# Attention with panel filler: one stretch of filler behind turn, outputs, scores and the second turned group

## The reference

```python
z = jnp.einsum('bhqd,bhkd->bhqk', q_blk, kh).astype(jnp.float32) * inv_sqrt
mask = key_pos[None, :] < q_pos[:, None]
log_1m_beta = jnp.where(mask, jax.nn.log_sigmoid(-z), 0.0)
suffix = lax.cumsum(log_1m_beta, axis=3, reverse=True) - log_1m_beta
a = jnp.where(mask, jnp.exp(jax.nn.log_sigmoid(z) + suffix), 0.0)
return jnp.einsum('bhqk,bhkd->bhqd', a, vh.astype(jnp.float32)).astype(q.dtype)
```

## Time and profile before

| | |
|---|---|
| Median of three runs | 2811.23 us |
| The profiled execution, its own time | 2811.8 us |
| Its span | 2810.0 us |
| PE busy | 2688.0 us, 96% of the span |
| PEld, DVE, ACT, POOL busy | 77%, 62%, 41%, 19% |
| The stage, 1481 to 1888 us: PE busy | 405.31 of 407 us |
| The stage: DVE, ACT busy | 202.35, 145.56 us |

### The profile page before, as it was taken

One profiled execution on the slowest core, in us unless ns is written; L12 is line 12 of the kernel. 1 busy time (PEld: TensorE's weight loads), 2 busy tenths in 40 slices (PEclk: granted clock), 3 DMA queues, 4 the chain that ended last, 5 costly groups with the idle time before them and its releaser, 6 DMA issues.

```text
span 2810.0 us, 39071 instructions
## 1 busy us (share of the span) xinstructions
PE 2688.0 (96%) x15746; PEld 2169.7 (77%) x15746; DVE 1731.8 (62%) x1998; ACT 1139.4 (41%) x2138; POOL 541.7 (19%) x434
## 2 busy tenths in 40 slices
PE   7999998999799999999799999999998999999997
PEld 6887566877788887888677777778877788888886
DVE  3467544563787778888815554531245765578889
ACT  3323564333777763333423333331016433333332
POOL 4322001348200000000432222213366000000002
PEclk9999999999999999999899999999999999999999
DMA  3210000004265655322411111221252323343323
GB/s 134 59 31 18 7 4 24 3 25 178 93 202 188 210 170 193 111 87 99 148 55 46 38 46 31 66 80 51 75 198 102 111 100 120 120 150 120 120 105 120
DMA packets 222604, 269.50 MB, mean 96 GB/s; under 512 B 16455, under 2 KB 158046, under 8 KB 222430
## 3 DMA queue, kind: packets, MB, share of 16 engines
q1 hardware_dynamic: 208174, 217.26, 23.9%
q10 hardware_dynamic: 14256, 49.81, 4.5%
HBM read 210.42 MB, written 56.62 MB: 95 GB/s over the span
## 4 chain that ended last, share of the span: by engine, by line
PE 80%; DVE 10%; POOL 3%; ACT 2%; issue 2%; DMA 2%; SPq 0%; ACTq 0%; DVEq 0%; POOLq 0%
PE ps L1647 7%; PE ps L1648 7%; PE ps L1649 7%; PE ps L1702 5%; PE ps L1704 5%; PE ps L1703 5%; PE ps L1761 4%; PE ps L1217 3%; PE ps L1219 3%; PE ps L1218 3%; PE ps L1763 3%; PE ps L1762 3%; PE ps L1438 3%; PE ps L1344 2%; PE ps L1236 1%
## 5 line engine op out<-in xcount | busy, mean ns | idle before, releaser
L1702 PE MATMUL ps<-down_t_hi,down_s_hi 128*128 128x512 f32 x896 | 349.5, 390 | 4.4 <-DVE acc L3205 2.2
L1704 PE MATMUL ps<-down_t_hi,down_s_lo 128*128 128x512 f32 x896 | 348.7, 389 | 0.0
L1703 PE MATMUL ps<-down_t_lo,down_s_hi 128*128 128x512 f32 x896 | 348.6, 389 | 0.0
L1043 POOL TENSOR_SCALAR mean_sq<-ssq 128x1 f32<-128x1 f32 x64 | 37.1, 580 | 1294.7 <-ACT squares_junk_ffn L1921 1242.2
L428 POOL TENSOR_TENSOR slab_lo<-raw,slab_hi 128x1024 fp32r<-128x1024 f32 (+2 forms) x108 | 256.1, 2371 | 9.0
L2385 ACT CAST down_s_hi<-down_a 128x2048 fp32r<-128x2048 f32 x56 | 107.2, 1915 | 370.4 <-PE ps L1704 328.1
L425 POOL TENSOR_SCALAR slab_hi<-raw 128x1024 fp32r<-128x1024 f32 (+2 forms) x108 | 114.6, 1061 | 624.0 <-issue 479.6
L1647 PE MATMUL ps<-act_hi,up_hi 128*128 128x512 f32 (+1 forms) x544 | 205.7, 378 | 6.1 <-issue 2.8
L1648 PE MATMUL ps<-act_lo,up_hi 128*128 128x512 f32 (+1 forms) x544 | 204.9, 377 | 0.0
L1649 PE MATMUL ps<-act_hi,up_lo 128*128 128x512 f32 (+1 forms) x544 | 204.8, 376 | 0.0
L1702 PEld LDWEIGHTS ps<-down_t_hi,down_s_hi 128*128 128x128 f32 x896 | 168.2, 188 | 42.6 <-issue 8.0
(11 more groups left out here) (365 smaller groups left out, 6173.0 us busy)
## 6 DMA issues: line engine op xcount, KB each, us to landing
down_a<-hid_spill SPq DMA_DIRECT2D x32, 1024.0 KB, 7.3
hid_spill<-up_hid ACTq DMA_DIRECT2D x30, 1024.0 KB, 6.4
raw<-in_w_in SPq DMA_DIRECT2D x56, 512.0 KB, 3.8
w_ada<-in_w_ada SPq DMA_DIRECT2D x48, 512.0 KB, 3.9
raw<-in_w_out SPq DMA_DIRECT2D x32, 512.0 KB, 3.8
up_raw<-in_w_up SPq DMA_DIRECT2D x16, 1024.0 KB, 5.4
down_b<-in_w_down SPq DMA_DIRECT2D x16, 1024.0 KB, 6.9
up_raw<-in_w_mlp_in SPq DMA_DIRECT2D x16, 1024.0 KB, 5.4
```

What stands on the lines that cost most here:

```text
L1702: pe.matmul(out, ops["s_hi"][:, k, cols], ops["t_hi"][:, k, :], start=first, stop=False, skip_group_check=True)
L1703: pe.matmul(out, ops["s_hi"][:, k, cols], ops["t_lo"][:, k, :], start=False, stop=False, skip_group_check=True)
L1704: mm = pe.matmul(out, ops["s_lo"][:, k, cols], ops["t_hi"][:, k, :], start=False, stop=last, skip_group_check=True)
```

## The change

In PE's `sb_step` the filler no longer stands in three pieces. Before: first turned group, three units, second turned group, two units, outputs, scores, the rest of the units. Now: first turned group, outputs, scores, second turned group, all six or seven units. No instruction is added or removed, no wait is changed, and the code of the other engines is the same.

```diff
                 if step >= SB_LAG_TURN:
                     pair, item = divmod(step - SB_LAG_TURN, SB_ITEMS)
                     sb_turn(pair, item, 0)
-                    mid_units(unit, unit + 3)
-                    if sb_pieces(item) == 2:
-                        sb_turn(pair, item, 1)
-                    mid_units(unit + 3, unit + 5)
-                    unit += 5
                 if step >= SB_LAG_PV and s % 2 == 0:
                     pair, item = divmod(step - SB_LAG_PV, SB_ITEMS)
                     sb_outputs(pair, item // 2)
...
                     elif s % SB_ROUND == 3 and i + 1 < SB_PAIRS:
                         sb_scores(i + 1, 0, 0)
+                if step >= SB_LAG_TURN and sb_pieces(item := (step - SB_LAG_TURN) % SB_ITEMS) == 2:
+                    sb_turn((step - SB_LAG_TURN) // SB_ITEMS, item, 1)
                 mid_units(unit, end)
```

## The result

| | before | after |
|---|---|---|
| Median (8 runs each) | 2810.77 us | 2818.35 us |
| Ratio, with its 95% interval | | 1.0026 (1.0016 to 1.0036) |
| The profiled execution's span | 2810.0 us | 2816.9 us |
| Step 2 to step 65, first transpose to first transpose | 392.30 us | 398.68 us |
| First transpose of step 2 to the first matmul of the next stage | 397.78 us | 405.03 us |

The changed kernel is slower by 7.6 us, 0.26%. The stage alone grew by 7.25 us in the profiled executions. What lies ahead of it took 0.7 us more and what lies behind it 1.0 us less, both without a change in the code. Steps that an edit does not touch repeat to some 0.03 us from one execution to another.

What follows compares the result with a forecast made beforehand. PE was taken as the bound, busy 2688 of 2810 us. Terms 5.6 + 1.1 + 1.2 - 0.4 - 2.35 gave 5.15 us slower, median 2816.4 us; range for 8 in 10 was 2812.5 to 2821.

Steps and rivals of the forecast that it cites:

- Scores that wait for betas: Early scores in steps 9, 23, 27, 37, 47, 51 and 61 wait for ACT's late betas; loss 5.6 us.
- Second group in second steps: Second turned group waits for ACT's copy behind narrow scores in steps 5, 17, 21, 33, 49; loss 1.1 us.
- Tail, steps 64 and 65: Second group waits for ACT's copy with only outputs or nothing between the groups; loss 1.2 us.
- The two waits that exist: PE's waits for ACT's copy in steps 32 and 48: the first stays, the second goes; gain 0.4 us.
- Edges: PE's borders between kinds of matmul: scores into transposes cost less than into filler; gain 2.35 us.
- I keep that wait: Step 32's second group: chain ends and group is due 0.5 us earlier alike, so its 1.45 us wait stays.
- the waits don't appear: Rival: PE reaches the scores later than placed, leaving the edges alone, 2809 us; chance 0.03.
- first steps wait too: Rival: second groups of first steps wait behind ACT's betas and DVE's mask; 7 us if seven run late, 2823; chance 0.15.
- Not slower: Rival: border from scores or outputs to transposes costs nothing, 4.3 us more gain; 2811 with shorter waits; chance 0.07.
- The clock falls: Rival: stretches of up to 2.8 us without filler run at 1.2 GHz, 45 us more, 2861; chance 0.01.
- signs of being wrong: First steps besides 32 wait, waits at scores sum under 4 or over 8 us, or stage and kernel grow differently.

Runs made afterwards that it cites:

- e1: Changed kernel with ACT's betas of second and fourth steps ahead of the taking of halves ended in the step before; 2812.64 us, ratio 1.0007.
- e4: Changed kernel with POOL's split of one slab cut to 8 of 1024 columns, so its result is incomplete; 2813.46 us, ratio 1.0011.
- e6: Changed kernel with DVE's convolution taps one step later, behind the products and mask of the next step; 2812.84 us, ratio 1.0012.
- e2: Changed kernel with one unit of filler behind the first turned group in every step; 2808.14 us, ratio 0.9991.
- e3: Changed kernel with scores of second and fourth steps back behind five units of filler; 2826.24 us, ratio 1.0059.
- e11: Kernel before, with DVE doing the first convolution tap of the third panel three times (two repeats); 2815.11 us, one run.

## Why the prediction was right, and where it was not

It said slower by 5.15 us, with even chances for more or less than 0.2%. It is slower by 7.6, inside the range, and the interval of the ratio reaches to both sides of 0.2%. No large errors cancel in the sum: four terms came within 0.5 us and one was 2.6 off. Its steps against the stage, which grew by 7.25 us with the last step:

| step of the prediction | forecast | measured | from |
|---|---|---|---|
| Scores that wait for betas | +5.6 | +5.5 | stage of after less e1 |
| Second group in second steps | +1.1 | +1.1 | steps 17, 33, 49: 0.30 each over their neighbours without a wait; 5, 21: 0.1 |
| Tail, steps 64 and 65 | +1.2 | +1.2 | 0.35, and 5.48 to 6.35 us from step 65 to the next stage |
| The two waits that exist | -0.4 | +2.2 | step 32: +2.54, step 48: -0.53, without edges |
| Edges | -2.35 | -2.8 | the rest of the sum; 0.09 in each of some 29 steps, little in the others |

The seven places of the first step and the order of their lengths were the ones forecast (step 27 shows no wait of its own, but is 0.14 us longer than in e1). The first two steps held because every cover could be read from one row, and everything behind PE's wait stood in PE's own queue. The scores did come earlier and with them the masks, as forecast, but outside steps 32 and 48 no wait of PE hung on that chain, so it bought nothing there. The reason given for step 48 was not the right one: its wait goes in e1 too, where step 47 is no longer than before.

The step that failed is "I keep that wait". I saw that the half on which the taps hang does not come earlier, and still let the chain end 0.5 us earlier, with each tap as long as in the rows of before. The chain ended 0.6 us later: the second group of step 32 came 4.68 us after the first, and not the 3.6 of the forecast (4.11 less 0.5). Two things made the 1.1 us. The taps had met POOL's split only in part and now meet all of it, 5.6 us instead of 4.8 (alone 3.35, e4). And they start 0.3 us earlier and not 0.5, because the half itself ends 1.9 us later against step 32, which used up the time that DVE had won. The wait grew by 1.2 us instead of staying, and behind it the clock cost another 1.6 us, which I had only as a rival in another form.

Of the rivals, "the waits don't appear" fell with the first row, and "first steps wait too" did not occur outside step 32. "Not slower" fell: scores into transposes keep a border. It can be read where the changed kernel has no wait, in step 25:

```profile
1627.07 0.92 PE L1785 MATMUL ps<-k_feat,q_feat 64*128 64x384 f32 x4
1627.91 0.44 PE L1804 MATMUL ps<-consts,sb_weights 128*128 128x128 f32 x2
1628.11 0.48 PE L1761 MATMUL ps<-act_hi,slab_hi 128*128 128x512 f32 x1
```

Two transposes behind scores take 0.20 us to the next start, 0.14 without a border (0.11 and 0.03), so 0.06 of border is left, as the prediction had taken it from the other attention's row. "The clock falls" happened, but in one place, behind a wait and not in the stretches without filler (e6), and for 1.6 us and not for 45. What was held against it, that the other attention was granted 1.00, holds for the window shown, but from 302 to 305 us of the same trace the clock was at 0.50. The Trainium skill's sentence on transposes and the gate (TensorE: Matmul & The Clock Gate, "Part 4: PE-mode transpose") is neither borne out nor refuted by that: up to 2.8 us of transposes, outputs and scores in a row kept the full clock. The Trainium skill's rule that a change of tiling mode drains the array (TensorEngine Tiling (Array Packing), "Key Properties") agrees with the border that stays, but not with a gain of nil: the border toward transposes is about half of that toward filler (0.06 and 0.11 us).

Of the forecast's signs of being wrong none showed: waits at scores sum to 5.2 us, no first step but 32 waits, and stage and kernel grew alike (7.25 and 7.6 us). What did not hold is that filler, transposes and scores keep their spacing; behind step 32's wait they did not.

One sentence of the prediction was plainly wrong and harmless: PE's functions for scores and turns stand ahead of the removed lines, so their line numbers did not change.

## What to carry to other kernels

Filler that looks movable on the engine that never waits is cover for particular waits. List what each instruction behind it waits for, and where that stands in the other engine's queue. Where a late part of another job stands ahead of it, that part sets the price. A little filler in the right place does: one unit of six (e2) made the stage 7.0 us shorter, more than the 6.4 us that moving them all had cost, and a place in ACT's queue (e1) took back 5.5 without any. When a wait is kept in a sum, read again which operations run beside its chain in the new order, and when the work it hangs on ends there.

## What the runs showed of the hardware

- PE's clock after a single wait: in step 32 waits of 0.40, 1.45, 1.93 and 2.24 us (one profiled execution each) left the granted clock at 1.00; waits of 2.65 (after), 2.66 (e1), 2.69 (e3) and 3.03 us (e11) were followed by a stretch at 0.50, with 512-column matmuls 0.43 us apart. It cost 1.6 us on top of the wait. But an equal wait of 1.93 us in the other attention was followed by 0.50 in ten executions of 13, so no length here is a bound below which the clock is safe.
- DVE beside POOL: two scalar_tensor_tensor operations of 128x1024 took 2.60 us alone and 4.59 us where the first 2.2 us of them ran beside POOL's subtraction of the same size; tensor_scalar took 0.75 us with POOL idle, 1.03 beside POOL's tensor_scalar and 2.17 beside its subtraction.
